# Start of a decoder layer on TensorE: shared squares, 64-column modulation products, high products first, index scores one unit later

## What is computed

```python
mod = silu(c) @ w_ada + b_ada                      # 1024 x 3072 weights, one vector
shift, scale, gate = split(mod, 3)
h = rmsnorm(x, norm_in) * (1 + scale) + shift      # needs the mean square of every token of x
proj = h @ w_in                                    # 4680 columns
...
score = sum over 8 heads of w_idx * relu(q_idx @ k_idx.T)   # per 128-query block, causal
sel   = top 256 keys of score                      # then sparse softmax attention over them
out   = rmsnorm(x + gate * (concat(y_conv, y_attn) @ w_out))
```

## Time and profile before

| | |
|---|---|
| device time, median of 3 runs | 722.95 us (721.53 to 723.73) |
| profiled execution, device time | 727.4 us |
| its span, first to last instruction | 725.2 us |
| mean granted TensorE clock | 0.976 of full |
| busy: PE / PEld / DVE / ACT / POOL | 673.8 / 556.9 / 468.8 / 372.0 / 220.4 us |

### The profile page before, as it was taken

One profiled execution on the slowest core, in us unless ns is written; L12 is line 12 of the kernel. 1 busy time (PEld: TensorE's weight loads), 2 busy tenths in 40 slices (PEclk: granted clock), 3 DMA queues, 4 the chain that ended last, 5 costly groups with the idle time before them and its releaser, 6 DMA issues.

```text
span 725.2 us, 8966 instructions
## 1 busy us (share of the span) xinstructions
PE 673.8 (93%) x3219; PEld 556.9 (77%) x3219; DVE 468.8 (65%) x772; ACT 372.0 (51%) x559; POOL 220.4 (30%) x109
## 2 busy tenths in 40 slices
PE   0889997999999999999999999998998999899996
PEld 0878986878888888888888877886777776678885
DVE  4675615577788899893069661013898989576734
ACT  6645634555663142452543345434888787865212
POOL 1001215422234152667756489420011110000000
PEclk9879998999999999999999999998999999999999
DMA  8870388353222111101100362075844440121531
GB/s 316 306 257 1 89 165 167 94 178 106 89 87 88 59 49 39 59 29 59 58 30 30 106 213 70 18 174 140 267 117 112 93 118 1 59 85 61 174 116 58
DMA packets 27910, 78.63 MB, mean 108 GB/s; under 512 B 3986, under 2 KB 8410, under 8 KB 27868
## 3 DMA queue, kind: packets, MB, share of 16 engines
q1 hardware_dynamic: 27524, 77.03, 35.7%
q10 hardware_dynamic: 344, 1.05, 0.6%
HBM read 61.25 MB, written 13.41 MB: 103 GB/s over the span
## 4 chain that ended last, share of the span: by engine, by line
PE 77%; DVE 9%; ACT 4%; issue 4%; DMA 3%; SPq 2%; ACTq 1%; DVEq 0%
PE ps L726 15%; PE ps L728 15%; PE ps L727 15%; PE ps L906 4%; PE ps L907 4%; PE ps L908 4%; PE ps L844 4%; PE ps L784 2%; PE ps L785 2%; DMA iqs<-hlL 2%; PE ps L765 2%; PE ps L766 2%; DVE acc L1328 2%; DVE phL L1535 2%; PE ps L858 1%
## 5 line engine op out<-in xcount | busy, mean ns | idle before, releaser
L726 PE MATMUL ps<-hH,wH 128*128 128x512 f32 (+1 forms) x544 | 212.5, 391 | 1.5 <-issue 1.4
L728 PE MATMUL ps<-hH,wL 128*128 128x512 f32 (+1 forms) x544 | 211.0, 388 | 0.0
L727 PE MATMUL ps<-hL,wH 128*128 128x512 f32 (+1 forms) x544 | 211.0, 388 | 0.0
L1687 POOL TENSOR_TENSOR wL<-raw,wH 128x1024 fp32r<-128x1024 f32 x35 | 85.7, 2448 | 188.4 <-ACT wH L959 188.4
L726 PEld LDWEIGHTS ps<-hH,wH 128*128 128x128 f32 x544 | 102.6, 189 | 21.8 <-issue 3.2
L728 PEld LDWEIGHTS ps<-hH,wL 128*128 128x128 f32 x544 | 102.6, 189 | 20.5
L727 PEld LDWEIGHTS ps<-hL,wH 128*128 128x128 f32 x544 | 102.7, 189 | 18.4
L1527 DVE CUSTOM_DVE_ANT_0 ps<-ps,bias 128x128 f32<-128x128 f32 (+3 forms) x64 | 48.7, 761 | 45.7 <-PE ps L766 43.7
L1535 DVE TENSOR_TENSOR phL<-ps,phH 128x512 fp32r<-128x512 f32 (+1 forms) x96 | 52.6, 554 | 23.0 <-ACT phH L1164 17.4
L1144 ACT ACTIVATE relu<-ps,wabs 128x384 f32<-128x384 f32 (+5 forms) x48 | 40.2, 848 | 45.1 <-PE ps L785 24.6
L1421 DVE SCALAR_TENSOR_TENSOR score<-relu,wsgn,score 128x384 f32<-128x384 f32 (+5 forms) x42 | 49.7, 1184 | 19.2 <-ACT relu L1144 16.7
(11 more groups left out here) (221 smaller groups left out, 1172.2 us busy)
## 6 DMA issues: line engine op xcount, KB each, us to landing
raw<-in_w_units SPq DMA_DIRECT2D x36, 512.0 KB, 3.3
ks<-qk_halves SPq DMA_DIRECT2D x32, 256.0 KB, 5.7
xin<-in_x SPq DMA_DIRECT2D x8, 512.0 KB, 7.9
wa<-in_w_ada SPq DMA_DIRECT2D x8, 512.0 KB, 11.8
wa<-in_w_ada SPq DMA_DIRECT2D x16, 256.0 KB, 4.9
gw<-in_w_ada SPq DMA_DIRECT2D x8, 512.0 KB, 3.7
qs<-qk_halves SPq DMA_DIRECT2D x16, 256.0 KB, 4.1
wo<-in_w_out SPq DMA_DIRECT2D x8, 512.0 KB, 9.3
```

The source lines that it names most:

```text
L726: pe.matmul(out, wH[slot(n)][:, kt, :], hH[:, kt, cols], start=(kt == 0), stop=False)
L727: pe.matmul(out, wH[slot(n)][:, kt, :], hL[:, kt, cols], start=False, stop=False)
L728: mm = pe.matmul(out, wL[slot(n)][:, kt, :], hH[:, kt, cols], start=False, stop=(kt == KT - 1))
L1687: g.tensor_tensor(wL[slot(n)][:], raw[slot(n)][:], wH[slot(n)][:].bitcast(F32), ALU.subtract).then_inc(s_wL, 1)
```

## The change

1. The squares of token tiles 4, 5 and 6 move from ACT to DVE (`tensor_tensor_reduce` into a new tile `squaresD`); the scaling of token tiles 6 and 7 moves from DVE to ACT. The root is taken in two groups of four. The token tiles are turned in groups of two. POOL's first low part of weights waits until DVE has written the two rotary tables.
2. Modulation products are 64 columns wide: the moving operand, a column, is broadcast, and only column 0 of each result is read. Those of channel tile 0 come first, complete. Parts 1 and 2 add all eight row blocks on DVE, so their products with `silu(c)` on PE are gone.
3. `wa1` and `wa2` change places, so that `wa1` no longer waits for the sums of part 0, and `wa2` does.
4. In the first units, all `hH` products of a channel tile stand ahead of its `hL` products, and the modulation products of parts 1 and 2 move to after unit 0's high products of channel tiles 3 and 5. On DVE, part 0's second `factors` go behind `first_low(1)`, the first sums of part 1 behind `low_h(1)`; on ACT, `tabC` and the weights of unit 2 change places.
5. Index scores of block i run one unit later, block 2 now in (`aq`,2), unit 8. The waits and relus on POOL and ACT move along.

```diff
-        ("ak", 0): [("idx", 2)],
-        ("aq", 1): [("idx", 3)],
+        ("aq", 1): [("idx", 2)],
+        ("aq", 2): [("idx", 3)],
...
-X_GROUPS = ((0, 4), (4, 6), (6, 8))
+TURN_GROUPS = ((0, 2), (2, 4), (4, 6), (6, 8))
+ACT_SQUARES = (0, 1, 2, 3, 7)
+DVE_SQUARES = (4, 5, 6)
+ACT_SCALES = (6, 7)
...
+    elif _kt in (3, 5):
+        FIRST_STEPS += _high[0:1] + [("mod", _kt, (_kt - 1) // 2)] + _high[1:3] + _low
+    else:
+        FIRST_STEPS += _high + _low
+SUMS = (KT - 1, KT, KT)
...
-                    if g == 1 and i == 0:
-                        sp.wait_ge(s_acc, SUMS)
+                    if g == 2 and i == 0:
+                        sp.wait_ge(s_acc, SUMS_END[0])
...
+                for first, last in ((0, 1), (1, n)):
+                    out = ps[:, bank + (first == 0), :]
+                    cols = [j for k in range(first, last) for j in (k, n + k)]
+                    for j in cols:
+                        mm = pe.matmul(out[:, MODW * j:MODW * j + MODW], sums[:, P * j:P * j + P], onesF[:].broadcast_to([P, MODW]),
+                                       start=(j == first), stop=(SUMS[g] == KT), skip_group_check=True)
...
-            for lo_t, hi_t in X_GROUPS:
-                for t in range(lo_t, hi_t):
-                    square(t)
...
+            for t in ACT_SQUARES[0:4]:
+                square(t)
...
+            act.wait_ge(s_rinv, 2)
+            for t in ACT_SCALES:
+                A(xin[:, t, :], xin[:, t, :], ACT.Copy, scale=rstd[:, t:t + 1]).then_inc(s_xnA, 1)
...
+            def square(t):
+
+                dve.wait_ge(s_x[x_sem(t)], 16)
+                if t - DVE_SQUARES[0] >= 2:
+                    dve.wait_ge(s_sqD, t - DVE_SQUARES[0] - 1)
+                v.tensor_tensor_reduce(squaresD[:, t % 2, :], xin[:, t, :], xin[:, t, :], 1.0, 0.0, ALU.mult, ALU.add,
+                                       sumsq[:, t:t + 1]).then_inc(s_sqD, 1)
...
-            factors(1, 6)
+            factors(1, 6, 0)
+            factors(1, 6, 1)
...
+            pool.wait_ge(s_wide, 2)
             split_low(0)
```

More of the change, by code:

```diff
@@ L150 @@
 X_TURNS = ((2, 2, 0), (3, 4, 0), (4, 6, 0), (5, 0, 0), (6, 2, 1), (1, 4, 2), (7, 6, 3), (0, 0, 4))
[L151 to L154, removed]
+FIRST_STEPS = []
+for _kt in range(KT):
+    _high, _low = [("high", _kt, n) for n in range(NFIRST)], [("low", _kt, n) for n in range(NFIRST)]
+    if _kt == 0:
+        FIRST_STEPS += _high[0:2] + _low[0:2] + _high[2:3] + _low[2:3]
+    elif _kt in (3, 5):
[3 more added lines that the diff above has]
+SUMS = (KT - 1, KT, KT)
+SUMS_END = tuple(sum(SUMS[0:g + 1]) for g in range(len(PARTS)))
+MODW = 64
 NF = ROPE // 2
@@ L686, in first_unit @@
                     cols = slice(S - w * (2 - half), S - w * (1 - half))
[L687 to L694, removed]
+                    if kind == "high":
+                        pe.matmul(out, wH[slot(n)][:, kt, :], hH[:, kt, cols], start=(kt == 0), stop=False)
+                        pe.matmul(out, wL[slot(n)][:, kt, :], hH[:, kt, cols], start=False, stop=False)
+                    else:
+                        mm = pe.matmul(out, wH[slot(n)][:, kt, :], hL[:, kt, cols], start=False, stop=(kt == KT - 1))
+                if kind == "low" and kt == KT - 1:
                     mm.then_inc(s_unit, 1)
@@ L701, in _ @@
             pe.wait_ge(s_amp, 2)
[L702 to L708, removed]
+            for kind, kt, n in FIRST_STEPS:
+                if kind == "mod":
+                    if n > 1:
+                        pe.wait_ge(s_amp, 2 * n)
+                    modulation(n, 6)
                 else:
-                    first_unit(*at_step)
+                    first_unit(kind, kt, n)
             def unit(n):
@@ L999, in _ @@
                 A(hH[:, kt, :], xT[:, kt, :], ACT.Copy).then_inc(s_hH, 1)
-                if kt == 0:
-                    split_high(2)
+                if kt == 1:
+                    act.wait_ge(s_tabp, 2)
+                    A(tabC[:], two(6), ACT.Copy).then_inc(s_tab, 1)
             split_high(NFIRST)
@@ L1351, in low_h @@
                 v.tensor_tensor(hL[:, kt, :], xT[:, kt, :], hH[:, kt, :].bitcast(F32), ALU.subtract).then_inc(s_hL, 1)
[L1353 to L1355 removed]
+            for t in DVE_SQUARES:
+                square(t)
+            inverse(0)
+            for t in (0, 1):
+                normalize(t)
+            inverse(1)
+            for t in (2, 3, 4, 5):
+                normalize(t)
+            for i in range(SUMS[0]):
                 ada_sum(0, i)
[L1357 removed]
+            factors(0, 2, 0)
             first_low(1)
[L1359 removed]
+            factors(0, 2, 1)
             low_h(0)
             first_low(2)
+            low_h(1)
+            ada_sum(1, 0)
             ada_sum(1, 1)
[L1363 removed]
             ada_sum(1, 2)
```

135 lines of the change are left out of this document (70 added, 65 removed).

## The result

| | before | changed |
| --- | --- | --- |
| median, us | 723.1 (721.5 to 726.2, 8 runs) | 727.9 (726.6 to 728.8, 8 runs) |
| ratio to before | | 1.0065 (95%: 1.0047 to 1.0083) |
| profiled execution's span, us | 725.2 | 726.4 |
| DVE's search, start of its first operation to start of its last, us | 108.3 | 121.4 |

The forecast was 711.0, in a range from 707 to 717.5. The time is outside it, and the kernel became slower where it was forecast to become faster. The ratio's interval lies wholly above 1.

What follows compares the result with a forecast made beforehand. PE, busy 93% of the span, and its waits were taken to bound the kernel. Terms of 5.8 and 6.4 us summed to 12.2, taken as 12.0: 722.95 - 12.0 = 711.0 us, range 707 to 717.5.

Steps and rivals of the forecast that it cites:

- With the clock full, PE starts products at 35.0: Kernel's head, after part 0's modulation: PE's first products start at 35.0, 2.9 us earlier than before.
- the transposes bring PE up to speed: Head: PE's transposes speed up at 21.75, so the modulation 0.3 us behind them was taken to hold full clock.
- first term: Head: ACT takes the key unit at 66.7, so unit 7 starts earlier, a gain of 5.8 us.
- Ready at 109.1, they hold a PE that comes at 107: Start of unit 7: its weights are ready at 109.1, PE arrives at 107 and waits about 2 us.
- The wait of 3.8 is gone, and so is the half clock behind it: First index scores, one unit later: the 3.8 us wait for `iqs` and 2.6 us of half-clock loss both go.
- 10.6 are left, and the cost is nothing: DVE's threshold search: scores end 11.1 us later against PE, 10.6 of 21.74 us slack remain, so no cost.
- Rival 4: DVE's threshold search over 23 us late, PE stops at L808, kernel slower (above 725.1 us); chance 0.03.
- second term: First index scores one unit later: wait for `iqs` and the half clock behind it removed, a gain of 6.4 us.

Runs made afterwards that it cites:

- c5: a2 with modulation products one column wide instead of 64: 725.3 us, ratio to before 1.0019.
- a2: Changed kernel with PE's wait for `tabC` moved from ahead of the first products to the modulation that overwrites its bank: 722.5 us, ratio to before 0.9979.
- a4: Changed kernel with the index scores put back where they stood before and PE's wait for `tabC` moved as in a2: 717.3 us, ratio to before 0.9910.
- a3: Changed kernel with ACT's relus of block 2 put ahead of the high part of `aq1`: 720.4 us, ratio to before 0.9970.
- c1: Changed kernel with the edits of both a2 and a3: 715.0 us, ratio to before 0.9871.
- d1: c2 with the gate's weight loads also one unit later and its column sums behind `az0`: 709.7 us, ratio to before 0.9812.
- c2: c1 with the two small transposes of the search's counts one unit later each: 719.0 us, ratio to before 0.9945.
- c3: Kernel before with only the index scores one unit later: 727.4 us, ratio to before 1.0061.
- b0: Kernel before, unchanged, run again for a second profile: 720.55 us (1 run).

## Why the prediction was wrong, by its own steps

- **"With the clock full, PE starts products at 35.0": failed.** Its parts held to about half a us (squares, scaling, sums of part 0 to 30.05, rows of 64 columns at 0.11 instead of 0.10 us, full clock through the modulation). That the width keeps the clock up is what c5 against a2 shows, one profile of each, and the other profiles agree with it. The prediction's reason, that the transposes bring PE up to speed, is not seen in the granted clock, which is 1.00 on both sides of 21.75; but after nothing but transposes the modulation did run at 1.00. What failed is that it counted what tile 0 needs, not what PE's program waits for: `pe.wait_ge(s_tab, 2)` stands ahead of the first product, and the change had moved `tabC` behind `hH` of tile 1. That is a wait of 3.75 us and some 6 us at half clock behind it, and unit 7 came 2.9 us earlier instead of 5.8. With the wait moved, the product is at 34.29 and the stage is better than forecast (key unit 64.7 against 66.7). a4 puts the head's worth at 6.5 us (4.1 to 8.8), where the first term said 5.8.
- **"Ready at 109.1, they hold a PE that comes at 107": right in kind.** PE waited about 1 us for unit 7's weights, at 112.03, as the rest came late.
- **"The wait of 3.8 is gone, and so is the half clock behind it": half failed.** `iqs` is no longer waited for. But the step took only `iqs` into account and not the order of ACT, on which the relus moved one unit past the high part of `aq1` and its wait for a spill. The new wait of 4.9 us is longer than the old. Putting the relus ahead (a3, c1) brings about 7.4 us. And the 2.6 us for the half clock were read from one execution; the second profile of before has none.
- **"10.6 are left, and the cost is nothing": failed.** The distance was right (read from the two traces, the search is 10.7 us later against PE) and the length was not. The delay pushes the search further into POOL's convolution work, which makes it 13.1 us longer: with the forecast's own terms, 21.7 - 11.1 - 13.1 - 1.2 (its last operation, 2.20 instead of 0.97) = -3.7, the wait that PE has. With its half clock it is worth about 5.3 us (c1 to d1, which moves the gate's loads too). Rival 4 named the place, but it looked for a DVE that falls behind by whole units and had a chance of 0.03. It came 14.3 us late, where 10.6 were free; the 23 us that it had as its own condition for a slower kernel assumed that all the rest would be gained.
- By the medians the three are worth 5.4 (a2), 7.4 (a3) and 5.3 (d1) us, 18.1 in all, against a miss of 16.9. The kernel with all three mended is at 709.7, close to the 711.0 forecast. That closeness is in part luck: 2.6 us of the second term came from a half clock that the second profile of before does not have, the head gave more than forecast, and d1 holds two moves that the forecast knew nothing of.

What stays open: why a wait of 3.5 us keeps the full clock in one profile of before and one of 3.8 does not in the other, and why one-column products kept it in c3; no run here varies either alone. Squares and scaling on two engines were not tried by themselves; their part of the head's gain is only read from the traces.

## What to carry to other kernels

When a block of work is moved later in a hand-written order, go through every in-order engine that takes part in it and list what it is now queued behind, waits included: two new stalls (the relus behind a spill, SP's weights behind the masks in c2) were such neighbours, and so was a semaphore ahead of the first product that had cost nothing while its signal was early. A slack of N us bears a delay of N only if the work in it keeps its length; ask what it will run beside at its new place. And read what a stall costs from more than one execution when the half clock behind it is a large part of its price.

## What the runs showed of the hardware

- DVE's operations on 128x6 elements take 0.16 us alone and stand still to the end of a wide operation of POOL that runs beside them (1.55, 2.32, 2.38 us). Its comparisons of 384 to 1024 columns did not: they take 61.6 or 61.7 us in all in every profile. The search lost 13.1 us to this in one change of place, and got 16.9 back when POOL had less to do.
- With modulation products of one column the granted clock fell to 0.50 while PE ran them in three profiles of four (both of before, c5), and in the fourth (c3) in a wait of 1.7 us right behind them. With 64 columns, at nearly the same distance of rows (0.11 us), it stayed at 1.00 through them in all nine profiles.
- The waits of PE looked at here, from 3.7 to 5.4 us long, were each followed by a stretch at 0.50 (behind the one of 3.72 us in the changed kernel a product takes 0.76 us instead of 0.39); the one of 3.5 us (b0) was not.
